# Two-layer transformer kernel: the sparse attention's softmax units regrouped from 24 to 16, one query projection moved between them

## The reference

```python
proj = h @ w_in                                # q (1024), six k/v sets (256 each), gates (48)
q = rotary(q, pos, 16, theta) * dh ** -0.5     # k_slc and k_win are rotated too
blocks = t[:, blk_idx] + pe                    # 15 blocks of 32 tokens, one every 16
kc, vc = rotary(gelu(blocks_k @ w1) @ w2), gelu(blocks_v @ w1) @ w2
p_cmp = softmax(q . kc, visible blocks)        # 15 keys
p_slc = softmax(q . ks, causal)                # all blocks are selected: 256 tokens
p_win = softmax(q . kw, window 512)            # causal, as there are 256 tokens
o = g0 * (p_cmp @ vc) + g1 * (p_slc @ vs) + g2 * (p_win @ vw)
return o @ w_out
```

## Time and profile before

| | |
|---|---|
| Median of three runs | 1344.35 us |
| Profiled execution, its own time | 1343.97 us |
| its span in the trace | 1342.2 us |
| TensorE busy | 1318.7 us, 98% |
| VectorE, ScalarE, GpSimd busy | 67%, 48%, 13% |
| The sparse attention's rounds, first score to last XL | 370.09 to 441.7 us |

### The profile page before, as it was taken

The page is one execution under the profiler, slowest core; times in us unless marked ns, Lnnn a source line. Parts: engine busy times, 40 slices in busy tenths (PEclk is TensorE's granted clock), DMA queues, the critical chain, the costliest instruction groups (busy, mean ns, idle before and its releaser), DMA issues.

```text
span 1342.2 us, 23944 instructions
## 1 busy us (share of the span) xinstructions
PE 1318.7 (98%) x9910; PEld 1186.9 (88%) x9910; DVE 899.3 (67%) x1382; ACT 641.6 (48%) x1121; POOL 180.2 (13%) x130
## 2 busy tenths in 40 slices
PE   9999999999989999999999999999999999999999
PEld 8989999999956899999978777888888888879999
DVE  6976777777868677766624556968775556775554
ACT  6655544444377554455433546332332346555552
POOL 0020111001210011110013000213122100301110
PEclk9999999999989999999999999999999999999999
DMA  8546676676600456655253200555556234414653
GB/s 315 198 157 206 221 263 221 225 242 207 201 10 2 162 201 232 206 190 189 95 180 111 101 33 32 173 168 178 169 161 196 87 125 139 145 58 158 208 190 127
DMA packets 64717, 217.49 MB, mean 162 GB/s; under 512 B 7136, under 2 KB 13152, under 8 KB 63968
## 3 DMA queue, kind: packets, MB, share of 16 engines
q1 hardware_dynamic: 60016, 208.69, 47.0%
q10 hardware_dynamic: 4592, 7.25, 1.5%
HBM read 210.68 MB, written 1.05 MB: 158 GB/s over the span
## 4 chain that ended last, share of the span: by engine, by line
PE 85%; DVE 8%; ACT 4%; issue 1%; DMA 1%; SPq 0%; POOL 0%; ACTq 0%; DVEq 0%; POOLq 0%
PE psum L332 24%; PE psum L333 23%; PE psum L334 23%; DVE WL L264 3%; PE psum L1254 2%; PE psum L1275 2%; ACT WH L259 1%; PE psum L329 1%; PE psum L331 1%; PE psum L330 1%; DMA stage<-ab_in 1%; PE psum L2701 1%; ACT arena L1367 1%; DVE arena L1325 1%; DVE SM L1301 1%
## 5 line engine op out<-in xcount | busy, mean ns | idle before, releaser
L332 PE MATMUL psum<-XX,WH 128*128 128x256 f32 (+1 forms) x1912 | 583.6, 305 | 8.2 <-DVE WL L264 2.8
L333 PE MATMUL psum<-XX,WH 128*128 128x256 f32 (+1 forms) x1912 | 574.7, 301 | 0.0
L334 PE MATMUL psum<-XX,WL 128*128 128x256 f32 (+1 forms) x1912 | 574.6, 301 | 0.0
L264 DVE TENSOR_TENSOR WL<-stage,WH 128x1024 fp32r<-128x1024 f32 x332 | 395.4, 1231 | 185.9 <-ACT WH L259 185.5
L259 ACT ACTIVATE WH<-stage 128x1024 fp32r<-128x1024 f32 x332 | 333.7, 1052 | 317.9 <-PE psum L334 272.8
L332 PEld LDWEIGHTS psum<-XX,WH 128*128 128x128 f32 x1912 | 358.9, 188 | 40.7 <-issue 14.5
L334 PEld LDWEIGHTS psum<-XX,WL 128*128 128x128 f32 x1912 | 358.9, 188 | 16.0
L333 PEld LDWEIGHTS psum<-XX,WH 128*128 128x128 f32 x1912 | 358.8, 188 | 15.5 <-issue 0.5
L2876 POOL TENSOR_TENSOR arena<-arena,con 128x512 f32<-128x512 f32 (+1 forms) x48 | 63.6, 1325 | 361.2 <-DVE con L2788 359.9
L332 PE MATMUL psum<-hidden,WH 128*128 128x256 f32 x352 | 97.5, 277 | 0.0
L334 PE MATMUL psum<-hidden,WL 128*128 128x256 f32 x352 | 97.2, 276 | 0.0
(11 more groups left out here) (291 smaller groups left out, 1739.6 us busy)
## 6 DMA issues: line engine op xcount, KB each, us to landing
stage<-w SPq DMA_DIRECT2D x132, 512.0 KB, 5.0
stage<-merge SPq DMA_DIRECT2D x80, 512.0 KB, 5.0
stage<-in SPq DMA_DIRECT2D x44, 512.0 KB, 4.7
arena<-ada SPq DMA_DIRECT2D x32, 512.0 KB, 4.1
stage<-ab_in SPq DMA_DIRECT2D x22, 512.0 KB, 6.2
stage<-nsa_in SPq DMA_DIRECT2D x20, 512.0 KB, 5.2
ring<-ada SPq DMA_DIRECT2D x16, 512.0 KB, 6.9
stage<-out SPq DMA_DIRECT2D x16, 512.0 KB, 4.4
```

Source lines behind the costliest of these rows:

```text
L264: e.tensor_tensor(lo, raw, hi.bitcast(F32), ALU.subtract).then_inc(s_lo, 1)
L332: e.matmul(dst, wh, xh, start=start, stop=False)
L333: e.matmul(dst, wh, xl, start=False, stop=False)
L334: return e.matmul(dst, wl, xh, start=False, stop=stop)
```

## The change

The 24 units become 16, in the order `t2`, `it`. For each pair (t2, it) there is one unit of 8 rows x 16 keys for both head pairs (br 0). In the first token tile each head pair has one unit of 8 rows x 128 keys, which holds branches 1 and 2 side by side (keys read through `N.kk`, two branches per matmul); in the second tile there are two units of 4 x 256 as before. The products with the compressed values move into the values of the next wide unit, with zero-padded vc tiles of 128 partitions (`n.vcs`: 16 products instead of 8, two banks, copied after the keys are rotated). `share` becomes a flag of a unit: the 8 x 128 units and those of branch 1 have half of the transposed copy on VectorE; branch 2 leaves all of it to ScalarE. q2 is projected where q3 was, and q3 in four quarters of 12 matmuls in TensorE's rounds 0, 0, 1 and 2; VectorE's share of q2 and q3 comes in rounds 0, 2 and 5, ScalarE's exchange of q3 in round 3. The blocks are made over two groups at a time, 16 additions of twice the size. The rest of the diff passes `u.T` and `u.before` in place of `T`, and moves the small sums in SM. The diff, cut to its core:

```diff
+        def scores_tensor(e, p, n, u, query, key, heads=None):
+
+            v, heads = scored(p, n, u), heads or u.hh
+            for h in range(heads):
+                to = h if heads == u.hh else slice(h, u.hh, heads)
                 for q in range(2):
                     r = slice(64 * q, 64 * q + 64)
-                    t = e.matmul(v[:, q, h, :], query(h)[r], key[r], start=h == 0 or u.mask is None, stop=u.mask is None)
+                    t = e.matmul(v[:, q, to, :], query(h)[r], key[r], start=h == 0 or u.mask is None, stop=u.mask is None)
...
-                    e.tensor_tensor(sm, sm, u.gate, ALU.mult).then_inc(*ve.tick())
+                    sb = sm.rearrange("p q (b h) -> p q b h", b=u.gate.shape[2])
+                    e.tensor_tensor(sb, sb, u.gate, ALU.mult).then_inc(*ve.tick())
...
-                if 2 <= n < N + 2 and share and units[n - 2].nj * units[n - 2].heads > 4:
-                    turned(e, ve, p, n - 2, units[n - 2], T, 512, 1024)
+                if 2 <= n < N + 2 and units[n - 2].share:
+                    turned(e, ve, p, n - 2, units[n - 2], 512, 1024)
...
+        N.gvp = view(13298, 960, "p (g c) -> p g c", g=4)
+        N.vcs = view(14480, 1024, "p (i d) -> p i d", i=16)
+        N.Tc = [view(15504 + 128 * n, 128) for n in range(2)]
+        N.kk = view(8064, 1024, "p (b t n) -> p t b n", b=2, t=2)
...
-        for it in range(2):
-            for t2 in range(2):
+        N.wide = []
+        for t2 in range(2):
+            for it in range(2):
+                gt = N.gt[:, it, :].rearrange("p (g h b) -> p g b h", g=4, h=4)[:, 2 * t2:2 * t2 + 2]
+                few = Unit(4, 16, 16, mask=endM[:, it * 16:it * 16 + 16], gate=gt[:, :, 0:1])
+                few.into(N.Tc[it], (2, 6)[it] if t2 else None)
+                N.units.append(few)
+                N.at.append((it, t2, None, 0))
                 for f in range(2):
-                    for br in range(3):
-                        gt = N.gt[:, it, :].rearrange("p (g h b) -> p g h b", g=4, h=4)[:, 2 * t2:2 * t2 + 2,
-                                                                                      2 * f:2 * f + 2, br]
-                        if br == 0:
-                            N.units.append(Unit(2, 16, 128, mask=endM[:, it * 16:it * 16 + 16], gate=gt))
-                        else:
-                            N.units.append(Unit(2, 128 * (it + 1), 256, mask=causalM, at=128 * it, gate=gt))
+                    for br in (1,) if it == 0 else (1, 2):
+                        g = gt[:, :, br:br + 2 - it, 2 * f:2 * f + 2]
+                        u = (Unit(4, 128, 128, mask=causalM, gate=g, share=True) if it == 0 else
+                             Unit(2, 256, 256, mask=causalM, at=128, gate=g, share=br == 1))
+                        n = len(N.wide)
+                        u.into(N.T[n % 2], N.wide[n - 2] if n >= 2 else None)
+                        N.wide.append(len(N.units))
+                        N.units.append(u)
                         N.at.append((it, t2, f, br))
+                    N.end[len(N.units) - 1] = 2 * t2 + f
+        N.steps = [[(m.count(n)) for n in range(len(N.units) + 3)] for m in ((0, 0, 1, 2), (0, 2, 5), (3,))]
+        N.last = [max(n for n, k in N.end.items() if k == i) for i in range(4)]
...
             fm(0, "n.q0")
             fm(1, "n.q1")
-            fm(2, "n.q2")
             w, n = ring_take(e, rings, 2048, "p (i m c) -> p i m c", i=2, m=16)
             e.wait_ge(*ve.of("n.blocks"))
...
             pe.mark(f"ring{n}")
-            fm(3, "n.q3")
+            fm(2, "n.q2")
...
-            b = tile(e, "n.vcs")
-            for i in range(8):
-                at = 80 * i - 16 * (i % 4)
-                t = e.matmul(b[0:64, i * 64:i * 64 + 64], N.gvp[:, at:at + 64], w2[:, 1, :], start=True, stop=True)
+            b = tile(e, "n.vcs", 2)
+            for i in range(16):
+                at = 112 - 16 * (i % 8)
+                t = e.matmul(b[:, i * 64:i * 64 + 64], N.gvp[0:64, 2 * (i // 8) + i % 8 // 4, at:at + 128], w2[0:64, 1, :],
+                             start=True, stop=True)
             t.then_inc(*pe.tick("n.vcs"))
             e.wait_ge(*ve.of("n.kcT"))
             rope_tensor(e, "nkc", N.kcT[:, :, 0:15], 2, C("p8"), n=15)
+
+            def later():
+                w = Chunk(flow, "nsa_in", 3)
+                b = tile(e, "n.q3", 1, (7,))
+                for h in range(2):
+                    for ks in (range(0, 4), range(4, 8)):
+                        for k in ks:
+                            t = product(e, b[:, h * 256:(h + 1) * 256], w, k, slice(h * 128, h * 128 + 128), XH[:, k, CTX],
+                                        XL[:, k, CTX], k == 0, k == 7)
+                        if h + ks[0] == 5:
+                            t.then_inc(*pe.tick("n.q3"))
+                            w.done()
+                        yield
+
...
                 if n == 0:
                     e.wait_ge(*ve.of("nkc.roped"))
+                    e.wait_ge(*ac.of("masks"))
+                if n == 1:
                     e.wait_ge(*gp.of("nkw.roped"))
-                    e.wait_ge(*ac.of("masks"))
                 if br == 0 and it == 0:
-                    e.wait_ge(*gp.of(f"nq{2 * t2 + f}.roped"))
+                    e.wait_ge(*gp.of(f"nq{2 * t2 + 1}.roped"))
...
-                scores_tensor(e, "n", n, N.units[n], lambda h: N.q[:, t2 * 4 + 2 * f + h, it * 128:it * 128 + 128],
-                              (N.kcT, N.ks, N.kw)[br][:, t2, 0:N.units[n].J])
+                key = (N.kcT[:, t2, 0:16] if br == 0 else N.kk[:, t2, :, 0:128] if it == 0 else
+                       N.kk[:, t2, br - 1, 0:256])
+                q0 = t2 * 4 + 2 * (f or 0)
+                scores_tensor(e, "n", n, N.units[n], lambda h: N.q[:, q0 + h, it * 128:it * 128 + 128], key,
+                              4 if br == 0 else 2)
...
+            def values(n):
                 it, t2, f, br = N.at[n]
                 if br == 0:
+                    held["few"] = n
+                    return
+                u = N.units[n]
+                if br == 1:
                     held[0] = tile(e, f"n.value{it}{t2}{f}", 1, (6, 7))
+                    few = held["few"]
+                    e.wait_ge(*ac.of(f"n.turned{few}"))
+                    if n == 1:
+                        e.wait_ge(*ve.of("n.vcs"))
+                    for q in range(2):
+                        for h in range(2):
+                            t = e.matmul(held[0][64 * q:64 * q + 64, h * 128:h * 128 + 128], N.vcs[:, 8 * t2 + 4 * q + 2 * f + h, :],
+                                         N.units[few].T, start=h == 0, stop=False)
                 b = held[0]
                 e.wait_ge(*ac.of(f"n.turned{n}"))
-                if N.units[n].nj > 1:
+                if u.share:
                     e.wait_ge(*ve.of(f"n.turned{n}"))
-                if n == 0:
-                    e.wait_ge(*ve.of("n.vcs"))
-                for jt in range(N.units[n].nj):
+                for i in range(2):
+                    jt, vs = (0, (N.vs, N.vw)[i]) if it == 0 else (i, (N.vs, N.vw)[br - 1])
                     for q in range(2):
-                        g = 2 * t2 + q
-                        if br == 0:
-                            for h in range(2):
-                                t = e.matmul(b[64 * q:64 * q + 64, h * 128:h * 128 + 128], N.vcs[:, 2 * g + h, :], T[:, 0:128],
-                                             start=h == 0, stop=False)
-                            continue
-                        v = (N.vs, N.vw)[br - 1][:, jt, g * 64:g * 64 + 64]
-                        t = e.matmul(b[64 * q:64 * q + 64, 0:256], v, T[:, jt * 512 + q * 256:jt * 512 + q * 256 + 256],
-                                     start=False, stop=br == 2 and jt == it)
+                        g, at = 2 * t2 + q, q * 512 + i * 256 if it == 0 else i * 512 + q * 256
+                        t = e.matmul(b[64 * q:64 * q + 64, 0:256], vs[:, jt, g * 64:g * 64 + 64], u.T[:, at:at + 256], start=False,
+                                     stop=i == 1 and (it == 0 or br == 2))
                 t.then_inc(*pe.tick(f"n.value{n}"))
...
-            held["out"] = Chunk(flow, "nsa_out", 0)
-
             def begin(j, ks):
+                if j + ks[0] == 0:
+                    held["out"] = Chunk(flow, "nsa_out", 0)
+                    held["b"] = tile(e, "n.begun", 2, (0, 2))
...
-            attend_tensor(e, "n", N.units, N.S, N.T, scores, values, iter(()), [0] * 27, last)
+            attend_tensor(e, "n", N.units, N.S, scores, values, later(), N.steps[0], last)
...
-                    for g in range(4):
-                        r = slice((g % 2) * 64, (g % 2) * 64 + 64)
+                    for q in range(2):
+                        r = slice(q * 64, q * 64 + 64)
                         for a in range(2):
                             for lh in range(2):
```

(42 more changed lines are left out.)

74 lines of the change are left out of this document (35 added, 39 removed).

## The result

The changed kernel takes 1358.57 us (median of four runs, 1356.01 to 1360.61), the kernel before 1345.59 beside it: a ratio of 1.0086 [1.0067, 1.0104]. By the ratio it is slower by 11.6 us, by the two medians as they stand by 13.0, where 3.9 were forecast; the median lies 6 us beyond the range.

The account below looks back on a forecast made before the run. TensorE, busy 98% of the span, was taken as the bound. Terms -0.4 - 0.7 + 1.4 + 3.4 + 0.2 = +3.9 on 1343.97, itself 0.4 under the median, gave 1347.9 us; range 1339.5 to 1352.5.

Parts of the forecast that it names:

- Blocks: Preamble: 16 additions of twice the size spare TensorE one wait and bring no new one; -0.4 us (0 to -0.4).
- q3 out, Gelus bare: Preamble: q3's projection leaves, -5.8 us; TensorE then idles for the uncovered Gelu chain ahead of `n.kcT`, +3.9.
- vcs: Preamble: `n.vcs` takes 16 products instead of 8, with twice the columns to load; +1.2 us (+1.1 to +1.7).
- term B: Preamble: q3's projection out, the Gelu wait and the longer vcs products together; -0.7 us (-0.7 to +0.3).
- Clock: Up to the first maximum: the dip comes earlier, +3.1 us there, and 1.7 go from the rounds; +1.4 (-1.7 to +4).
- q3 in the rounds: First rounds: q3's quarters fill TensorE's idle time, +2.3 us, scaling and exchange around them +1.1; +3.4 (0 to +6.9).
- Rounds: Sparse attention: less TensorE work, but finishes waiting for XH ahead of wide maxima; +0.2 us (-9 to +3).
- the signs set down for being right: TensorE idle 3 to 4 us before `n.kcT`, early dip, first score near 370.1, finishing rounds 3.8 to 4.2, last XL 444 to 446.
- the second one: First rounds: q3's quarters only delay the chain, 1351.4 us, or 1353.6 with two more GpSimd stalls; chance 0.16.
- The first one: Sparse attention: rounds follow TensorE's work and the finish costs nothing, -9 us there, 1338.7 in all; chance 0.16.
- The third: The clock stays up, or dips where nothing waits: -1.7 us for the clock, 1344.8 in all; chance 0.18.
- The warning: More than one clock dip, or TensorE idle over 1.5 us in a late round, would mean a cause not priced.

Follow-up runs that it names:

- w1: The changed kernel with only the last two block additions moved ahead of q0's scaling on VectorE; 1355.36 us, ratio 1.0056 to the kernel before.
- k2: The changed kernel with both Gelus ahead of the high part, and odd vcs products on rows 64 to 127 and in another bank; 1348.26 us, one run.
- k3: The changed kernel with 15 unread identity products filling TensorE's wait ahead of `n.kcT`; 1352.07 us, ratio 1.0055 to the kernel before.
- u1: The changed kernel with q2 and q3 projected ahead of the rounds, as in the kernel before; 1352.64 us, ratio 1.0047.
- c1: The changed kernel with maximum ahead of finish, Gelus ahead of the high part, last two block additions earlier, vcs behind the key rotation's product; 1350.51 us, ratio 1.0015.
- u2: The changed kernel with q2 and q3 ahead of the rounds, finish behind the maximum, block additions earlier, vcs behind the key rotation's product; 1346.38 us, ratio 0.9996.
- c2: c1 with VectorE's copy and rotation of `n.kcT` ahead of q1's rotation product, the low part and q2's scaling; 1346.97 us, ratio 0.9998.
- m1: The kernel before, old units and blocks, with only q3's projection, exchange and rotation moved into the first rounds; 1356.38 us, ratio 1.0080.
- f1: The changed kernel with VectorE's maximum of the next unit ahead of the finish in the sparse attention's rounds; 1352.85 us, ratio 1.0043.
- r1: The changed kernel measured again, unaltered, to see what repeats; 1355.64 us, ratio 1.0077 to the kernel before.
- b2: The kernel before with the finish behind the maximum and its 8 vcs products behind the key rotation's product; 1348.22 us, ratio 1.0000.
- u4: u2 with vcs in round 0, its copy in round 1, and VectorE's rotation products for q2 and q3 in rounds 3 and 5; 1348.39 us, ratio 1.0008.
- k1: The changed kernel with 28 unread identity products put into TensorE's wait ahead of `n.kcT`; 1359.08 us, ratio 1.0076.
- u5: u2 with eight of the 16 vcs products moved into round 1 and their copy into round 3; 1342.19 us (12 runs), ratio 0.9970.

## Why the prediction was wrong

Measured, the stage gained 10.7 us for 3.9 forecast. By the steps of the prediction:

- **Blocks** (-0.4, "I see no new wait"): the saving came, the wait of 0.38 is gone, but a new one came with it. The last two additions do stand right behind q0's scaling, but that scaling itself comes behind a low part and ends after q1 does. TensorE waited 1.58, and w1 took 2.4 out of the stage. I had their place and did not compute their time.
- **q3 out, Gelus bare** (-5.8 + 3.9): right to the tenth; the wait is 3.88, ended by the second Gelu.
- **vcs** (+1.2, range +1.1 to +1.7): 3.78 at full clock for 1.12 before, +2.7. I scaled from eight products that used all 128 rows; k2 shows that half the rows, all sixteen in the same half and bank, are nearly twice as dear as halves in turn. (With the range that I gave vcs, term B is -0.8 to -0.2, not -0.7 to +0.3.)
- **Clock** (+1.4): the dip did begin where I put it, behind the Gelu wait. That the 3.1 us that I gave for what lies in it is near the 2.9 of k3 is luck in part: vcs alone lost 2.3 of the 2.9, and the first wide scores ran slow in k3 as well. Wrong was the credit of 1.7 for a dip moved away from the rounds: of the low clock, which went from 10.2 to 23.9 us, 17 lie behind the first score, where all of the 10.2 lay, since the rounds have idle times of their own and the clock fell twice more.
- **q3 in the rounds** (+3.4): right as a sum; 3.0 (changed against u1), 3.1 (c1 against u2), 3.6 (c2 against u2). Its split into 2.3 for the quarters and 1.1 around them was not tested, and the rotation was not the hidden work that I took it for: some 1.1 us of the idle time at 404.61 come with its sine product. With the old units it was 5.9 (m1), inside the bounds given.
- **Rounds** (+0.2, range to +3): this is the step that failed most, at +3.3 (u1 98.2 against 94.9). The mechanism was the one named, a finish that waits for XH ahead of a wide maximum, and two finishing rounds in a row came as priced: from 395.86 to 399.69 it is 3.83 us, for 4.0. What failed is the price of the round behind them, which I put at 3.7 as if nothing were handed on. The delayed maximum delays the exps (3.8 us of waits behind finishes in the changed kernel, 4.3 in u1), these the next XH and the scale, and TensorE's turn comes late: the turns at 399.11 and 404.61 are 5.50 us apart. The same ones are 4.32 apart in f1 (maximum first), 4.41 in u1 (without q3's part) and 3.51 in u2 (both). The clock fell there as well. f1 takes 6.6 us away by order alone, and u2 is 6.6 under u1 behind the first score, with vcs and the blocks reordered too.

The steps' sum with the measured terms: 1.6 - 0.4 - 5.8 + 3.9 + 2.7 + 2.9 + 3.0 + 3.3 = 11.2, 0.5 more than the 10.7 found; the difference lies within what one kernel's stage differs by from run to run (1.3, r1). The last two terms are differences of the same traces, so that only the terms ahead of the first score are tested by this sum. Of the signs set down for being right, the wait for the Gelu and the two finishes 3.8 us apart came; the first score did not (4.5 us later in the stage, not within 1), nor the last XL at 444 to 446 (451.5). The prediction's rivals: the second one (slower, 1351.4) had the sign, but for q3's quarters, which cost what the forecast gave them. The first one (rounds that follow TensorE) was the potential that the finish's place hid: behind the first score u2 is 3.3 under the kernel before and b2 is not. The third is refuted by three dips. The warning that more than one dip, or over 1.5 us of idle time in a late round, would mean an unpriced cause held on both counts.

The rule of the Trainium skill that I weighed (TensorE: Matmul & The Clock Gate, The HAM clock gate), that activity releases the throttled state, agrees with k3, where activity in place of an idle time kept the clock up to the first score. It did not make q3's quarters worth anything: the first began at 378.2 at 1.2 GHz, the clock was back 2.4 us later, and the two later dips came all the same. The other rule of the Trainium skill (SBUF — State Buffer, Who interferes with whom), that a VectorE instruction with two SBUF inputs and a GpSimd instruction that reads SBUF get in each other's way, agrees with u2's first two rounds, where two gate products took 1.22 us instead of 0.17. Moving them in u4, where the longest took 0.64, brought nothing that the intervals show.

## What to carry to other kernels

Before moving a piece of work out of a stretch, list what it covered and compute when each of those chains ends, the last link included; here two of them came bare, for 5.5 us. Fewer, wider units pay only if nothing that waits stands ahead of the instruction that starts the next unit: the same units cost 3.3 us with the finish ahead of the maximum and, the rest also in order, gained 3.3 with it behind. And an idle time on TensorE can cost more than itself: ahead of `n.kcT` 3.5 us of products that nobody reads brought the first score 2.9 us forward. It pays only inside the wait; k1's, too long by 2.5, gave it all back.

## What the runs showed of the hardware

**Two paces at full clock.** At a granted clock of 1.00 and with no waits, the same matmuls follow each other at two paces. Two kernels alike up to there, at 200 us; the kernel before:

```profile
200.01 0.28 PE L332 MATMUL psum<-XX,WH 128*128 128x256 f32 x1
200.12 0.28 PE L333 MATMUL psum<-XX,WH 128*128 128x256 f32 x1
200.24 0.28 PE L334 MATMUL psum<-XX,WL 128*128 128x256 f32 x1
```

and c1:

```profile
200.12 0.28 PE L332 MATMUL psum<-XX,WH 128*128 128x256 f32 x1
200.24 0.28 PE L333 MATMUL psum<-XX,WH 128*128 128x256 f32 x1
200.35 0.28 PE L334 MATMUL psum<-XX,WL 128*128 128x256 f32 x1
```

Averaged over 40 us these are 0.1133 and 0.1178 us apart, 4%. c1's trace keeps the slower one from 130 to 305 us and reaches L367 at 311.5 instead of 304.8. In the last layer it is the changed kernel that has it; the same 20 us of its program and of before's (busy us, instructions):

```profile
1280.00:1300.00 20.00, 20.00 (x172) 20.00 (x172) 11.27 (x14) 10.55 (x15) 2.54 (x4) 1.00 0.61 199
```

```profile
1280.00:1300.00 20.00, 20.00 (x179) 20.00 (x178) 11.93 (x15) 9.83 (x15) 3.29 (x5) 1.00 0.57 183
```

172 matmuls for 179. From the last L367 (1092.9 before, 1102.8 changed) to the end this makes some 4 us, which is most of the difference between the spans (13.8) and the stage (10.7). It isn't the change's: of the eighteen traces b2 has the slow pace there with the old units, and u2 and k2 the fast one with the new. What sets the pace I don't know. That it makes the times of one kernel differ is likely: beside u5, the kernel before had 12 runs of 1342.0 to 1345.7 us and 15 of 1346.9 to 1349.0. It was not tested.

**Row halves.** Sixteen fp32 products with 64 rows and 128 columns of weights took 3.78 us with all weights in the same rows and 2.00 with alternating ones and two banks.
